# A decoder step on one core: both value products of a head pair issued one behind the other, behind the next unit's transposes

## The chip, the cores and the metric

The kernel is written in Bass for one core of a Trainium2 chip. It is one launch that fills five instruction queues by hand: TensorE (PE), ScalarE (ACT), VectorE (DVE), GpSimd (POOL) and SyncE (SP). Each queue runs in order, and semaphores tie them together. The metric is the device time of one launch in microseconds. The kernel before took 1098.66 us in the median of 3 runs (1098.1 to 1100.58). The execution that was profiled took 1095.08 us.

## The reference, cut to what matters

One hybrid decoder layer is computed for a prompt of 1024 tokens and for 8 samples of 8 tokens each, with the same weights. The part that matters here is the attention of the prompt. There are 8 blocks of 128 queries. For every block there are 8 NSA heads (two KV heads of four query heads each) with three branches, and 4 heads of attention into 256 memory tokens. Selection of blocks is no restriction here, since there are only 16 blocks and the 16 best are taken.

```
def gathered_attend(qb, kg, vg, mask):
    s = jnp.einsum('bqkgd,bkqsd->bkgqs', qb, kg) * SCALE
    p = masked_softmax(s, mask[:, :, None])
    return jnp.einsum('bkgqs,bkqsd->bqkgd', p.astype(vg.dtype), vg)

def window_attend(qb, t, kw, vw, kpos):
    s = jnp.einsum('bqkgd,bskd->bkgqs', qb, kw) * SCALE
    mask = (kpos[None, :] <= t[:, None]) & (kpos[None, :] > t[:, None] - WINDOW) & (kpos[None, :] >= 0)
    p = masked_softmax(s, mask)
    return jnp.einsum('bkgqs,bskd->bqkgd', p.astype(vw.dtype), vw)
```

In all branches the scores, the softmax and the product with the values are separate steps, and the results are `gates * o_c + gates * o_s + gates * o_w`. Around this part lie the input projection and the retention heads (the first 510 us), and the output projection with the last RMSNorm (the last 130 us).

## The kernel before, in words

**Units.** The prompt's attention is cut into NV = 144 units, 18 for each of the 8 query tiles (`UN = 18`). Tile i is the units 18i to 18i+17. A unit v holds the softmaxes of one head. Units come in pairs: the even unit v and the odd unit v+1 are the same branch for head g of the first KV head and head g of the second. Units 0, 1 of every four are the selected branch (i+1 key tiles of 128), units 2, 3 are the window branch (up to 5 key tiles) together with the compressed branch (one tile of 64 keys). The last two units of a tile (16, 17) hold the memory heads, two each.

**What is done for a unit.** On PE `qk(v)` computes scores into one of two PSUM areas (lines 1473, 1474, and 1476 for the mask). On DVE `maxima(v)` takes the row maximum (line 1798). On ACT the exponential writes the probabilities P[v % 2] into SBUF (line 1722). PE transposes the tiles of P in chunks of up to four tiles (line 1500) into PSUM bank 4 + c % 3, where c counts all chunks. ACT or DVE, in turns, copies a chunk out to one of six buffers PT (line 1661). PE then multiplies the values with the PT chunks of both units of a pair (line 1623), one chunk of the even unit with the same chunk of the odd unit: that is `pv(pair)`. When a group of six results is complete, ACT copies it out (`ot`, line 1748), PE transposes it back (chunk kind "o", line 1505), and DVE normalises it (`norm`, lines 1809 to 1814).

A pair of units has one chunk each, or two. The selected branch has two chunks from tile 4 on, the window branch from tile 3 on. In the text, C0 and C1 are the first and second chunk of an even unit, and A0, A1 and B0, B1 those of the even and the odd unit of the pair before it. pv(A0, B0) and pv(A1, B1) are the two products of that pair.

**What sets the order.** `schedule()` (line 1191 and on) writes one list of steps, and every engine walks through it and issues its part. For a unit v the steps are: `qk(v + 2)`; the chunks of v, each with `add_p`; the `pv` that are due; `sm(v + 2)`, which is maxima and exponential of the unit v + 2; then one group of steps of other work: transposes of the next tile's queries (chunk kind "q", line 1510, whose two-part copy is ACT line 1735 and DVE line 1891), or the samples' attention (kinds "mk", "kt", "st", "si", "sv" and so on, lines 1530 to 1598). These other chunks use the same three banks.

**The waits that matter.** A transposed chunk c waits until the chunk c - 3 was copied out of its bank. `qk(v + 2)` waits until the exponentials of unit v are done. `pv` waits until its chunks were copied. A copy into PT waits for the product that read that buffer six chunks ago. ACT and DVE run their steps in the list's order too.

**Where the change is.** Lines 1244 to 1256, in the loop over a unit's chunks. `waiting` is the list of pairs whose product is not issued yet, and `ranks` numbers the chunks of kind "p". Before, at most one product was issued behind each chunk, and only when the pair's last chunk lay two or more such chunks back.

Of the kernel before, what the change touches and what calls it, by code (L numbers as in the profile page):

```python
# [144 lines left out]
def build(nc, io):  # L145
# [1008 lines left out]
    def softmaxes(v):  # L1154

        i, l = v // UN, v % UN
        base = 1024 * (v % 2)
        if l >= 16:
            m = l - 16
            return [(24 + 2 * m + j, 24 + 2 * m + j, 3, 2 * m + j, 0, NM, [(base + 512 * j, NM)], 256 * j) for j in range(2)]  # L1160
        g, j = l // 4, l % 2
        h, k0 = g + 4 * j, 0 if l % 4 < 2 else max(0, i - WIN // 128)
        n = 128 * (i + 1 - k0)
        halves = [(base, n)] if n <= 512 else [(base, n // 2), (base + 512, n // 2)]
        if l % 4 < 2:
            return [(6 * g + j, 6 * g + j, 0, h, 0, n, halves, 0)]
        return [(6 * g + 2 + 2 * j, 6 * g + 2 + j, 1, h, k0, n, halves, 0), (6 * g + 3 + 2 * j, 6 * g + 4 + j, 2, h, 0, 64, [(base + 512 + 448, 64)], 640)]

    def tiles_of(v):

        return [(a, k, min(128, s[5])) for a, s in enumerate(softmaxes(v)) for k in range((s[5] + 127) // 128)]

    def sample_groups():

        groups = [[("t", ("sq",))]]
        for g in range(2):
            groups += [[("t", ("mk", b))] for b in range(4 * g, 4 * g + 4)]
            groups += [[("t", ("mq", g))], [("me", g)], [("t", ("mt", g))], [], [("t", ("mv", g)), ("load_mem", 1) if g == 0 else ("load_pair", 0)], [("store_mem", g)]]
        for p in range(NPAIR):
            groups += [[("t", ("sc", p))], [("ec", p)], [("nc", p)], [], [("t", ("si", p))]]  # L1180
            groups += [[("t", ("kt", p, c))] for c in (4, 5)]
            groups += [[("t", ("sw", p))], [("mw", p), ("t", ("kt", p, 0))], [("ew", p), ("t", ("kt", p, 2))], [("t", ("ss", p, 0))],
                       [("t", ("kt", p, 1))], [("t", ("kt", p, 3))], [("t", ("st", p, 2))], [("t", ("ss", p, 1))], [("ms", p)], [("es", p)],
                       [("t", ("st", p, 3))], [("t", ("st", p, 0))], [("t", ("st", p, 1))], [("t", ("sv", p))] + ([("load_pair", p + 1)] if p + 1 < NPAIR else []),
                       [("store_pair", p)]]
        groups += [[("load_fin", 0)], [], [("fin", 0)], [], [], [("load_w", 0)], [("load_w", 1)], [], []]
        for m in range(4):
            groups += [[("w_hi", m)], [("w_lo", m)] + ([("load_w", m + 2)] if m < 2 else []), []]
        return groups

    def schedule():

        chunks, steps, waiting, outs = [], [], [], []
        act_of, turn, ranks = [], [0], {}

        def add(c):  # L1200
            kind = c[0]
            copied = kind in ("p", "mk", "mt", "kt", "st")
            act_of.append(turn[0] % 2 == 0 if copied else kind == "sw")
            turn[0] += copied
            chunks.append(c)
            steps.append(("t", len(chunks) - 1))

        def add_p(v, tiles):
            add(("p", v, tiles))
            c = len(chunks) - 1  # L1210
            ranks[c] = len(ranks)
            for o in outs:
                o[1] += 1
            while outs and outs[0][1] >= 2:
                write(outs.pop(0)[0])
            return c

        def write(n):
            add(("o", n))
            steps.append(("norm", n))  # L1220

        def pv():
            pair = waiting.pop(0)
            steps.append(("pv", pair))
            v = chunks[pair[1]][1]
            a, k, _ = chunks[pair[1]][2][-1]
            if v % UN in (3, 7, 11, 15, 17) and a == 1 and 128 * (k + 1) >= softmaxes(v)[a][5]:
                n = NG * (v // UN) + (v % UN) // 4
                steps.append(("ot", n))
                outs.append([n, 0])  # L1230

        groups = sample_groups()
        first = 4
        for part in range(3):
            add(("q", 0, part))
        steps.append(("load_q", 2))
        for v in range(2):
            steps.extend([("qk", v), ("sm", v)])
        for v in range(NV):
            i, l = v // UN, v % UN  # L1240
            if v + 2 < NV:
                steps.append(("qk", v + 2))
            tiles = tiles_of(v)
            mine = []
            for f in range(0, len(tiles), 4):
                mine.append(add_p(v, tiles[f:f + 4]))
                if waiting and ranks[waiting[0][1]] + 2 <= ranks[mine[-1]]:
                    pv()
                if l >= 16:
                    waiting.append((mine[-1], mine[-1]))  # L1250
                elif l % 2:
                    waiting.append((partner[len(mine) - 1], mine[-1]))
            partner = mine
            if v + 2 < NV:
                steps.append(("sm", v + 2))
            if i >= 1 and i + 1 < QT and l == 5:
                steps.append(("load_z", i + 1))
            if i + 1 < QT and l in (9, 11, 13):
                add(("q", i + 1, (l - 9) // 2))
                if l == 13 and i + 3 < QT:  # L1260
                    steps.append(("load_q", i + 3))
            for what, n in groups.pop(0) if v >= first and groups else []:
                if what == "t":
                    add(n)
                else:
                    steps.append((what, n))
            if v == 2 * UN:
                steps.append(("copy_win", 0))
            if v % 4 == 0 and 2 * UN < v <= 2 * UN + 24:
                steps.append(("copy_kv", (v - 2 * UN) // 4 - 1))  # L1270
            if v == NV - 8:
                steps.extend([("load_m", 0), ("load_m", 1)])
            if v >= NV - 2:
                d = v - (NV - 2)
                steps.append(("load_x", d))
                for part in range(2):
                    add(("x", d, part))
        assert not groups
        for d in range(NT):
            steps.append(("d", d))  # L1280
            if d + 2 < NT:
                steps.append(("load_m", d + 2))
            if d == 0:
                while waiting:
                    pv()
                while outs:
                    write(outs.pop(0)[0])
            if d + 2 < NT:
                for part in range(2):
                    add(("x", d + 2, part))  # L1290
            steps.append(("y", d))
            if d + 2 < NT:
                steps.append(("load_x", d + 2))
        return chunks, steps, act_of

    p_chunks, p_steps, p_act = schedule()

    def chunk_act(c):
# [757 lines left out]
```

## Time and profile before

| | |
|---|---|
| median of 3 runs | 1098.66 us (1098.1 to 1100.58) |
| profiled execution | 1095.08 us, its span 1093.3 us |
| PE busy | 988.1 us, 90% of the span |
| DVE busy | 512.1 us, 47% |
| ACT busy | 390.4 us, 36% |
| POOL busy | 209.5 us, 19% |
| granted TensorE clock, mean | 0.973 of full |
| chain that ended last | PE 69%, DVE 8%, issue 7%, DMA 5%, ACT 5% |

"Busy" of PE counts the modelled time of matmuls, which overlap, so 90% busy is not 90% of what the array can do. PEld is the loading of weights, which is a row of its own: most matmuls here have one load each, and in a stream the loads stand end to end. "Issue" is time in which an engine waited for nothing that the profile shows. The time outside the span (1.8 us) is the same kind of overhead in any run. Times below are microseconds from the span's start. The prompt's attention runs from 514 to about 965.

### The profile page before, as it was taken

How to read it: one execution, taken by the hardware profiler on the slowest of the kernel's cores; microseconds unless marked ns; L12 is line 12 of the kernel's file. 1: busy time of each engine (PE TensorE's matmuls, PEld its weight loads, DVE VectorE, ACT ScalarE, POOL GpSimd, SP SyncE). 2: the span in 40 equal slices, each digit the busy share in tenths (PEclk: the TensorE clock that was granted, in tenths of full speed). 3: DMA queues.
4: the chain of work that ended last, by engine and by line, in shares of the span. 5: the costliest groups of instructions: out<-in, count | busy, mean ns of one | idle time of the engine just before them, and what ended most of it. 6: DMA issues, size and time to landing. Idle time of an engine off the chain costs nothing.

```text
span 1093.3 us, 20913 instructions
## 1 busy us (share of the span) xinstructions
PE 988.1 (90%) x8117; PEld 853.2 (78%) x8117; DVE 512.1 (47%) x1241; ACT 390.4 (36%) x961; POOL 209.5 (19%) x318
## 2 busy tenths in 40 slices
PE   1999999999999999998767888989898998999994
PEld 1999999999999999898555566666665776768883
DVE  4763332322225433362346557666655657634432
ACT  4432221142110121133335455555555557632210
POOL 1122221311152455412002012020010232002000
PEclk9999999999999999999689899999999999999997
DMA  7453431432425333173634484240330133013430
GB/s 197 158 196 101 143 114 62 143 76 95 128 71 138 110 116 102 35 175 103 158 108 123 139 271 114 56 156 1 91 98 1 52 97 128 18 49 125 147 123 38
DMA packets 100675, 119.15 MB, mean 109 GB/s; under 512 B 38770, under 2 KB 82706, under 8 KB 100002
## 3 DMA queue, kind: packets, MB, share of 16 engines
q1 hardware_dynamic: 88962, 78.44, 25.3%
q0 software_dynamic: 8704, 32.43, 8.5%
q10 hardware_dynamic: 2912, 6.95, 1.8%
q8 instruction: 65, 1.06, 0.4%
q14 instruction: 32, 0.26, 0.1%
HBM read 92.72 MB, written 32.02 MB: 114 GB/s over the span
## 4 chain that ended last, share of the span: by engine, by line
PE 69%; DVE 8%; issue 7%; DMA 5%; ACT 5%; SPq 3%; POOL 2%; ACTq 0%; DVEq 0%; POOLq 0%
PE psum L501 10%; PE psum L502 9%; PE psum L503 9%; PE psum L1500 4%; PE psum L1623 4%; PE psum L1473 3%; DVE p_nb L1798 3%; PE psum L1639 3%; PE psum L1640 3%; PE psum L1641 3%; ACT p_P L1722 2%; PE psum L1474 2%; PE psum L723 2%; PE psum L725 2%; PE psum L724 2%
## 5 line engine op out<-in xcount | busy, mean ns | idle before, releaser
L501 PE MATMUL psum<-a_whi,f_xhi 128*128 128x256 f32 (+2 forms) x968 | 279.8, 289 | 0.0
L502 PE MATMUL psum<-a_wlo,f_xhi 128*128 128x256 f32 (+2 forms) x968 | 274.2, 283 | 0.0
L503 PE MATMUL psum<-a_whi,f_xlo 128*128 128x256 f32 (+2 forms) x968 | 273.3, 282 | 0.0
L501 PEld LDWEIGHTS psum<-a_whi,f_xhi 128*128 128x128 f32 (+1 forms) x968 | 178.2, 184 | 2.7 <-issue 0.9
L502 PEld LDWEIGHTS psum<-a_wlo,f_xhi 128*128 128x128 f32 (+1 forms) x968 | 178.2, 184 | 0.0
L503 PEld LDWEIGHTS psum<-a_whi,f_xlo 128*128 128x128 f32 (+1 forms) x968 | 178.1, 184 | 0.0
L1722 ACT ACTIVATE p_P<-psum,p_nb 128x640 f32<-128x640 f32 (+7 forms) x224 | 123.8, 557 | 138.9 <-DVE p_nb L1798 128.5
L638 POOL DMA_DIRECT2D h_scratch<-a_hst x117 | 64.5, 553 | 262.5 <-DVE a_hst L940 176.8
L1500 PE MATMUL psum<-f_ident,p_P 128*128 128x128 f32 (+1 forms) x656 | 108.3, 285 | 5.9 <-DVE p_QB L1891 4.8
L1798 DVE TENSOR_REDUCE p_nb<-psum 128x1 f32<-128x640 f32 (+7 forms) x224 | 109.7, 520 | 4.3 <-PE psum L1476 3.3
L1661 DVE COPY p_PT<-psum 128x512 f32<-128x512 f32 (+4 forms) x108 | 56.3, 521 | 92.5 <-PE psum L1500 92.1
L1473 PE MATMUL psum<-p_KS,p_QA 128*128 128x320 f32 (+5 forms) x192 | 78.4, 409 | 12.1 <-ACT p_P L1722 9.8
L1623 PE MATMUL psum<-p_PT,p_V 128*64 128x128 f32 x1056 | 79.8, 284 | 0.9 <-ACT p_PT L1661 0.9
L1500 PEld LDWEIGHTS psum<-f_ident,p_P 128*128 128x128 f32 (+1 forms) x656 | 70.3, 142 | 12.8 <-DVE p_QB L1891 6.3
L1951 POOL TENSOR_TENSOR p_zt<-f_OC,p_zt 128x256 f32<-128x256 f32 x8 | 5.8, 724 | 384.5 <-DVE p_Oi L1814 384.5
L949 DVE TENSOR_TENSOR c_ctlo<-psum,c_cthi 128x512 fp32r<-128x512 f32 (+1 forms) x40 | 25.4, 636 | 106.1 <-ACT c_cthi L853 106.1
L1661 ACT COPY p_PT<-psum 128x512 f32<-128x512 f32 (+4 forms) x108 | 55.5, 514 | 41.4 <-PE psum L1500 41.2
L1623 PEld LDWEIGHTS psum<-p_PT,p_V 128*64 128x64 f32 x1056 | 56.1, 137 | 18.0 <-issue 15.8
L853 ACT CAST c_cthi<-psum 128x512 fp32r<-128x512 f32 (+1 forms) x40 | 21.8, 544 | 124.7 <-PE psum L706 124.7
L1474 PE MATMUL psum<-p_KS,p_QB 128*128 128x320 f32 (+5 forms) x192 | 64.3, 336 | 0.0
L1473 PEld LDWEIGHTS psum<-p_KS,p_QA 128*128 128x128 f32 x192 | 38.1, 199 | 30.9 <-ACT p_P L1722 16.5
L1639 PE MATMUL psum<-d_whi,d_xh 128*128 128x512 f32 (+1 forms) x144 | 57.6, 400 | 0.0
(290 smaller groups left out, 1757.8 us busy)
## 6 DMA issues: line engine op xcount, KB each, us to landing
a_wraw<-in_w_in SPq DMA_DIRECT2D x24, 512.0 KB, 5.4
h_scratch<-a_hst POOLq DMA_DIRECT2D x96, 128.0 KB, 2.1
s_SG<-in_cache_nsa_slc SPq DMA_DIRECT2D x64, 128.0 KB, 2.2
a_xraw<-in_x_prompt SPq DMA_DIRECT2D x8, 512.0 KB, 3.5
p_qd<-h_scratch SPq DMA_DIRECT2D x16, 256.0 KB, 3.9
s_MK<-in_cache_mem SPq DMA_DIRECT2D x8, 512.0 KB, 5.7
mix_scratch<-p_zt POOLq DMA_DIRECT2D x8, 512.0 KB, 3.0
s_WG<-in_cache_nsa_win SPq DMA_DIRECT2D x8, 512.0 KB, 5.8
```

Source lines behind the costliest of these rows:

```text
L501: nc.tensor.matmul(out, hi, wh, start=first, stop=False)
L502: nc.tensor.matmul(out, hi, wl, start=False, stop=False)
L503: return nc.tensor.matmul(out, lo, wh, start=False, stop=last)
L638: pool.dma_start(dst, hst[n % HST][0:r, 0:w]).then_inc(S(f"h_out{n % HST}"), 16)
L1473: nc.tensor.matmul(o, QA[i % 2][:, hq, :], k, start=True, stop=False)
L1474: l = nc.tensor.matmul(o, QB[i % 2][:, hq, :], k, start=False, stop=not masks)
L1500: l = nc.tensor.transpose(o[0:w, 128 * j:128 * j + 128], P[v % 2][:, at:at + w], ident[:])
L1623: i_mm = nc.tensor.matmul(psum[64 * j:64 * j + 64, at:at + 128], val, PTs[p_rank[pair[j]] % NPT][0:w, 128 * p:128 * p + 128], start=k == 0 ...
L1639: nc.tensor.matmul(o, hi, dwhi[jj][:, k], start=k == 0, stop=False)
L1661: copy(PTs[r % NPT][0:w, 0:128 * n], bank(4 + c % 3)[0:w, 0:128 * n]).then_inc(sem, 1)
L1722: nc.scalar.activation(dst, s_view(s), ACT.Exp, bias=nb[:, g % NNB:g % NNB + 1], accum_out=ssum[:, i % 2, s[1]:s[1] + 1]).then_inc(S("p_ex ...
L1798: nc.vector.tensor_reduce(out=nb[:, g % NNB:g % NNB + 1], in_=s_view(s), op=ALU.max, axis=AX.X if len(s[6]) == 1 else AX.XY, negate=True). ...
```

## The change

The product is no longer issued inside the loop over chunks. Behind all chunks of a unit, products are issued as long as there are any that don't need a chunk of this same unit, and only if the unit is even within its tile, or one of the two memory units.

```diff
             for f in range(0, len(tiles), 4):
                 mine.append(add_p(v, tiles[f:f + 4]))
-                if waiting and ranks[waiting[0][1]] + 2 <= ranks[mine[-1]]:
-                    pv()
                 if l >= 16:
                     waiting.append((mine[-1], mine[-1]))
                 elif l % 2:
                     waiting.append((partner[len(mine) - 1], mine[-1]))
             partner = mine
+            while waiting and (l % 2 == 0 or l >= 16) and waiting[0][1] not in mine:
+                pv()
             if v + 2 < NV:
                 steps.append(("sm", v + 2))
```

The first place is a window unit with two chunks in tile 6, on PE. p_P_118 are the probabilities of the even unit, p_PT_132 and p_PT_128 the copied chunks A0 and B0, p_PT_143 and p_PT_129 the chunks A1 and B1. Before:

```order
L1500 MATMUL psum<-f_ident,p_P_118 128x128 x4
L1623 MATMUL psum<-p_PT_132,p_V 64x128
L1623 MATMUL psum<-p_PT_128,p_V 64x128
...
L1500 MATMUL psum<-f_ident,p_P_118 128x128
L1500 MATMUL psum<-f_ident,p_P_118 64x128
L1623 MATMUL psum<-p_PT_143,p_V 64x128
L1623 MATMUL psum<-p_PT_129,p_V 64x128
...
L1582 MATMUL psum<-f_ident,s_PSl 128x128 x4
```

The same place now:

```order
L1500 MATMUL psum<-f_ident,p_P_118 128x128 x5
L1500 MATMUL psum<-f_ident,p_P_118 64x128
L1623 MATMUL psum<-p_PT_132,p_V 64x128
L1623 MATMUL psum<-p_PT_128,p_V 64x128
...
L1623 MATMUL psum<-p_PT_143,p_V 64x128
L1623 MATMUL psum<-p_PT_129,p_V 64x128
...
L1582 MATMUL psum<-f_ident,s_PSl 128x128 x4
```

The first product moved from between C0 and C1 to behind C1, and stands directly ahead of the second product. There are 32 such places, all in tiles 4 to 7.

The second place is a pair with one chunk per unit, in tile 1, on PE. p_P_118 and p_P_119 are the probabilities of the even and the odd unit, p_PT_128 and p_PT_129 the copied chunks of the pair before. Before:

```order
L1500 MATMUL psum<-f_ident,p_P_118 128x128 x2
L1473 MATMUL psum<-p_KS,p_QA_115 128x256
L1474 MATMUL psum<-p_KS,p_QB_117 128x256
L1476 MATMUL psum<-p_maskb,f_identb 128x128
L1473 MATMUL psum<-f_KCp,p_QA_115 128x64
L1474 MATMUL psum<-f_KCp,p_QB_117 128x64
L1476 MATMUL psum<-p_maskb,f_identb 128x64
L1500 MATMUL psum<-f_ident,p_P_119 128x128 x2
L1623 MATMUL psum<-p_PT_128,p_V 64x128
L1623 MATMUL psum<-p_PT_129,p_V 64x128
```

The same place now:

```order
L1500 MATMUL psum<-f_ident,p_P_118 128x128 x2
L1623 MATMUL psum<-p_PT_128,p_V 64x128
L1623 MATMUL psum<-p_PT_129,p_V 64x128
...
L1473 MATMUL psum<-p_KS,p_QA_115 128x256
L1474 MATMUL psum<-p_KS,p_QB_117 128x256
L1476 MATMUL psum<-p_maskb,f_identb 128x128
...
L1500 MATMUL psum<-f_ident,p_P_119 128x128 x2
```

The product moved from the odd unit up into the even unit, ahead of the next scores. With it the copy of finished results on ACT (line 1748) and the "o" transposes (line 1505) come one unit earlier in these tiles.

The third place is the end of tile 5 on PE, with the two memory units. p_PT_130 and p_PT_131 are memory chunks, and p_VM is the memory's values. Before, the product with p_PT_143 and p_PT_129 stands in the second memory unit, and both memory products in the first unit of the next tile:

```order
L1623 MATMUL psum<-p_PT_128,p_V 64x128
L1473 MATMUL psum<-p_KS,p_QA_114 128x448
...
L1500 MATMUL psum<-f_ident,p_P_119 128x128 x4
L1623 MATMUL psum<-p_PT_143,p_V 64x128
L1623 MATMUL psum<-p_PT_129,p_V 64x128
...
L1500 MATMUL psum<-f_ident,p_P_118 128x128 x4
L1623 MATMUL psum<-p_PT_130,p_VM 64x128 x4
L1500 MATMUL psum<-f_ident,p_P_118 128x128 x3
L1505 MATMUL psum<-f_ident,p_OT 128x128 x3
L1623 MATMUL psum<-p_PT_131,p_VM 64x128 x4
```

The same place now:

```order
L1623 MATMUL psum<-p_PT_143,p_V 64x128
L1623 MATMUL psum<-p_PT_129,p_V 64x128
...
L1473 MATMUL psum<-p_KS,p_QA_114 128x448
...
L1500 MATMUL psum<-f_ident,p_P_119 128x128 x4
L1623 MATMUL psum<-p_PT_130,p_VM 64x128 x4
...
L1500 MATMUL psum<-f_ident,p_P_118 128x128 x4
L1505 MATMUL psum<-f_ident,p_OT 128x128 x3
L1500 MATMUL psum<-f_ident,p_P_118 128x128 x3
L1623 MATMUL psum<-p_PT_131,p_VM 64x128 x4
```

Every product moved up by one place, and the "o" transposes stand between the two chunks of the next tile's first unit. The queues of SP and POOL are unchanged.

## Rows read from the trace of the kernel before

**Rows 1.** Busy time by stretch: PE, PEld, DVE, ACT, POOL, granted clock, DMA share, GB/s.

```profile
514.00:640.00 126.00, 96.03 (x775) 71.18 (x775) 65.68 (x207) 58.21 (x206) 13.85 (x24) 0.84 0.51 146
718.00:965.00 247.00, 222.96 (x2075) 167.43 (x2076) 154.53 (x338) 137.32 (x340) 31.80 (x31) 1.00 0.21 64
965.00:1093.00 128.00, 112.85 (x553) 88.58 (x549) 44.33 (x100) 25.04 (x53) 10.70 (x15) 0.96 0.29 103
```

**Rows 2.** Waits, 514 to 640: engine, waited for, total us, times, longest.

```profile
PE psum L1530 <- DMA s_MK<-in_cache_mem: 10.7, 2, 7.9
```

**Rows 3.** Waits of the weight loads, 718 to 965, same columns.

```profile
PEld psum L1623 <- issue: 13.9, 80, 0.2
PEld psum L1473 <- ACT p_P L1722: 9.8, 16, 1.4
PEld psum L1500 <- DVE p_QB L1891: 5.8, 6, 1.9
PEld psum L1500 <- issue: 4.8, 27, 0.3
```

**Rows 4.** Time line around one window unit of tile 6: start, us, engine.

```profile
873.42 0.42 PEld L1500 LDWEIGHTS psum<-f_ident,p_P 128*128 128x128 f32 x4
874.01 0.85 PEld L1623 LDWEIGHTS psum<-p_PT,p_V 128*64 128x64 f32 x16 [0.17 <-issue]
874.01 1.09 PE L1623 MATMUL psum<-p_PT,p_V 128*64 128x128 f32 x16
874.03 0.94 DVE L1798 TENSOR_REDUCE p_nb<-psum 128x1 f32<-128x640 f32 x2
875.04 0.17 PEld L1500 LDWEIGHTS psum<-f_ident,p_P 128*128 128x128 f32 x2 [0.17 <-issue]
875.04 0.44 PE L1500 MATMUL psum<-f_ident,p_P 128*128 128x128 f32 x2
875.51 0.42 DVE L1661 COPY p_PT<-psum 128x256 f32<-128x256 f32 x1 [0.53 <-PE psum L1500]
875.85 1.08 DVE L1798 TENSOR_REDUCE p_nb<-psum 128x1 f32<-128x896 f32 x1
878.18 0.19 PEld L1473 LDWEIGHTS psum<-p_KS,p_QA 128*128 128x128 f32 x1 [0.33 <-ACT p_P L1722]
```

**Rows 5.** Time line of the weight loads, 869 to 872.

```profile
869.97 0.19 PEld L1623 LDWEIGHTS psum<-p_PT,f_VC 64*64 64x64 f32 x4 [0.17 <-issue]
871.43 0.76 PEld L1500 LDWEIGHTS psum<-f_ident,p_P 128*128 128x128 f32 x7
```

**Rows 6.** Time line, the three units whose second chunk came late.

```profile
756.63 0.17 PEld L1500 LDWEIGHTS psum<-f_ident,p_P 128*128 128x128 f32 x2 [1.66 <-DVE p_QB L1891]
...
819.35 0.42 PEld L1500 LDWEIGHTS psum<-f_ident,p_P 128*128 128x128 f32 x4
821.54 0.69 DVE L1891 SCALAR_TENSOR_TENSOR p_QB<-psum,p_QA 128x512 fp32r<-128x512 f32 x1 [1.80 <-ACT p_QA L1735]
822.28 0.17 PEld L1500 LDWEIGHTS psum<-f_ident,p_P 128*128 128x128 f32 x2 [1.49 <-DVE p_QB L1891]
...
839.58 0.17 PEld L1500 LDWEIGHTS psum<-f_ident,p_P 128*128 128x128 f32 x2 [1.91 <-DVE p_QB L1891]
```

**Rows 7.** Time line, weight loads of scores that waited, first and last of seven.

```profile
797.04 0.19 PEld L1473 LDWEIGHTS psum<-p_KS,p_QA 128*128 128x128 f32 x1 [0.68 <-ACT p_P L1722]
...
940.14 0.19 PEld L1473 LDWEIGHTS psum<-p_KS,p_QA 128*128 128x128 f32 x1 [0.94 <-ACT p_P L1722]
```

**Rows 8.** Time line, one of seven units whose bank came free at the last moment.

```profile
886.04 0.42 PEld L1500 LDWEIGHTS psum<-f_ident,p_P 128*128 128x128 f32 x4
886.15 0.56 DVE L1814 TENSOR_TENSOR p_Oi<-psum,p_rw 128x384 f32<-128x384 f32 x1
```

**Rows 9.** Time line in tile 0: copy of an odd unit's chunk, next transposes.

```profile
518.80 0.29 DVE L1661 COPY p_PT<-psum 128x128 f32<-128x128 f32 x1 [1.02 <-PE psum L1500]
519.29 0.64 PE L1500 MATMUL psum<-f_ident,p_P 128*128 128x128 f32 x2
```

## The prediction

> **What bounds the kernel now.** I read the busy time by stretch first. The clock is granted in full from 718 to 965, PE is busy 223.0 of 247 us there, DVE 154.5 and ACT 137.3 [rows 1]. So PE is nearly the bound in tiles 4 to 7, but not alone: the waits of that stretch show the loads of scores standing 9.8 us for the exponentials, and the loads of transposes 5.8 us for a bank that DVE empties [rows 3]. From 514 to 640 PE is busy only 96.0 of 126 us at a mean clock of 0.84, and single waits for memory loads are as long as 7.9 us [rows 1, 2]. What is gained ahead of such a wait is lost at it. From 965 on the rest is mostly PE work [rows 1], and a shift of its start passes to the end.
>
> Then the time line of one window unit with two chunks. Four loads of transposes end at 873.84, and the first load of the product stands at 874.01, behind 0.17 of idle. The product's 16 loads take 0.85, and the next transposes start at 875.04, behind 0.17 again [rows 4]. The matmuls start with their loads (874.01 and 875.04), so the gap delays the array as well, and is not hidden under a matmul. That gap comes where the array's shape changes, 128*128 to 128*64 or back. It also comes inside one product, from 128*64 to 64*64, where there is no semaphore to wait for; and seven transposes that belong to two chunks, with waits between them, load in 0.76 without a gap [rows 5]. So it is the shape and not the wait that costs.
>
> **The change part by part.**
>
> *Changes of shape.* In the 32 units with two chunks of tiles 4 to 7, C0, product, C1, product becomes C0, C1, product, product. That is one entry into the narrow shape and one exit fewer. Over the whole order there are 114 runs of products before and 79 now; counting every boundary between full, half and quarter shape, there are 62 fewer. The profile has 27 exits towards transposes with 4.8 us of idle, 0.18 each [rows 3], and 0.17 in the unit shown [rows 4]. I take 62 times 0.17 = 10.5 us of PE time.
>
> The Trainium skill has two rules on this that point apart. "TensorEngine Tiling (Array Packing)", section Key Properties, says that changing the tiling mode drains TensorE. "TensorE: Matmul & The Clock Gate", in its opening table, says that the queue pulls weight loads ahead of matmuls in flight. By the first the sum stays as it is, by the second the loads behind a change would be ready and the gain would be nothing; the rows agree with the first.
>
> *C1 loses its cover.* C1 must wait until the chunk three back has left its bank. Before, the first product lay in between and hid 0.85 + 2 x 0.17 = 1.19 us of this. In 28 of the 32 units C1 did not wait at all, beyond the gap. In three it did: the waits of 1.66, 1.49 and 1.91 at 756.63, 822.28 and 839.58 [rows 6]. There the bank holds a chunk of queries, which needs a copy on ACT and then one on DVE: at 821.54 DVE starts, 1.8 us after C0's loads ended at 819.77 [rows 6]. This copy does not depend on where the product stands. So C1 starts when it did, and the product's 0.85 comes on top: 3 x 0.85 = 2.6 us lost. Their six gaps lay inside the waits and give nothing, 1.0 us less. The remaining unit of the 32 waited for a copy that its product waited for too, and does not change.
>
> *Who waits behind.* A PE wait at C1 holds both products, then the sample transposes and the next scores, and on ACT the copy of finished results (line 1748) with the exponentials behind it. This is in the 0.85.
>
> *C1 comes earlier.* In the other units C1 starts 1.02 earlier. Its copy stands ahead of the next even unit's maximum on DVE: the chain copy at 875.51, maximum 875.85, then exponential and, at 878.18, the scores that waited 0.33 for it, hangs on it [rows 4]. Here DVE had another maximum until 874.97 [rows 4], so half of the 1.02 would arrive. In tiles 5 to 7 scores issued in an even unit, whose exponentials hang on such a chain, waited seven times for over half a microsecond, 7.6 us in all [rows 7]. Bounds: nothing comes back, or all 7.6. I take a third, 2.5, since in most of these the chain hangs on other work of ACT or DVE too.
>
> *Gains that a later wait takes.* 56 gaps x 0.17 = 9.5 us are gone, but PE runs into its waits for ACT and DVE [rows 3] sooner, and there the gain stays only if the releaser came earlier as well. Bounds: nothing is taken, or all 9.5. I take 3.4, somewhat over a third, since PE waits in about every second pair.
>
> *Tiles 0 to 3.* The product moves from the odd into the even unit. Its chunks must be copied by then. The tightest place is in tile 0: the copy ends at 519.09, and the two transposes behind which the product now stands start at 519.29 and are issued by 519.6, so 0.5 us is left [rows 9]. The "o" transposes, copy and normalisation move with it, in the same sequence. I cost this at nothing; the cover is the time of the scores between. If it is gone, 24 such pairs that miss by 0.1 cost 2.4 us, part of which a memory wait swallows [rows 2].
>
> *Sum.* -9.5 + 2.6 + 3.4 - 2.5 = -6.0 us against the profiled 1095.08, so 1089.1. The median of the runs shown lies 3.6 higher than that execution, and I give the forecast on the median: 1098.66 - 6.0 = 1092.7. "Same" below means within 0.2%, 2.2 us, which is about what a measurement of this kernel can tell.
>
> **The rivals.**
>
> *Everything pays.* All 9.5 of gaps stays, and the earlier C1 removes most of the waits of its chain: -9.5 + 2.6 - 5 = about -12, or 1086.7. For it speaks that PE is the busiest by far [rows 1]; against it that DVE and ACT hold PE up in the same tiles [rows 3].
>
> *The gain is swallowed.* PE, DVE and ACT are close to a common rhythm, and all 9.5 are taken back at the next waits: 2.6 - 2.5 = about zero, 1098.8. For it speaks that the waits on ACT and DVE come every few units [rows 3].
>
> *The banks become the bound, and it is slower.* The three late units are not the only ones near the edge. In seven the bank came free less than 0.4 before C0's loads ended, or just behind: in the one shown the normalisation ends at 886.71, and C0's loads at 886.46 [rows 8]. If PE gets ahead of DVE, all ten expose the product: 10 x 0.85 = 8.5 lost, and 20 gaps worth 3.4 fall inside waits, so 7.1 is left of the 10.5. With 3.4 swallowed as above that is +8.5 - 7.1 + 3.4 = +4.8, or 1103.5. It decides when the bank comes free later than C0's end; up to there C1 costs nothing, and from a whole product's length later the full 0.85 is lost. Against it speaks that in most of the seven PE itself starts the copy, two or three blocks earlier, so that it would move along.
>
> *The change does not do what it says.* If the gap came from the wait ahead of each product, both gaps would stay between the two products and in front of C1, and only the 2.6 would be left: 1101.3. Rows 5 speak against it.
>
> **How the numbers follow.** Forecast 0.46, everything pays 0.23, swallowed 0.16, banks 0.11, not what it says 0.04. The forecast's own range is 1089 to 1097, from a sum with the two thirds halved or doubled. The range for 8 in 10 takes in most of "everything pays" and half of "swallowed": 1085 to 1100. Faster by over 0.2% is nearly all of the first two and a little of the third: 0.70. Same is the middle of "swallowed" and the upper edge of the forecast: 0.17. Slower is the last two: 0.13.
>
> **What would show it.** Right: the idle of L1500 put down to issue between 718 and the end of this stretch falls from 4.8 to near nothing, that of L1623 falls by some 27 entries from 80, transposes load in groups of five to eight, and the time line shows 24 or more narrow loads in a row. Three waits of about 2.5 us stand ahead of C1 where queries were transposed before. The stretch of tiles 4 to 7 is some 5 us shorter, the one after 965 unchanged in length. Wrong: more than five waits over 1 us ahead of C1, or a product that waits for its copy in tiles 0 to 3, or loads that keep their 0.17 between two products; any of these turns the sign or takes the gain.

## The result and the profile after

| | before | after |
|---|---|---|
| median | 1098.37 us (16 runs) | 1091.30 us (16 runs) |
| lowest, highest | 1094.77, 1104.25 | 1088.13, 1096.65 |
| profiled execution | 1095.08 | 1088.52 |
| its span | 1093.3 | 1086.7 |

The ratio of after to before is 0.9933, with a 95% interval of 0.9915 to 0.9951. That is 7.4 us less, 5.4 to 9.3. The two spans differ by 6.6.

The busy time of the changed kernel by stretch answers to [rows 1]; the columns are the same.

```profile
514.00:640.00 126.00, 95.38 (x768) 70.15 (x768) 65.01 (x205) 57.68 (x203) 14.24 (x25) 0.84 0.48 138
718.00:965.00 247.00, 220.07 (x2135) 173.30 (x2134) 157.37 (x343) 140.92 (x353) 31.75 (x31) 1.00 0.23 70
965.00:1086.00 121.00, 106.67 (x494) 84.06 (x492) 41.41 (x94) 21.44 (x43) 10.69 (x15) 0.96 0.27 98
```

In the same 247 us PE, DVE and ACT get through more: PE 2135 matmuls instead of 2075. Its busy time is nevertheless 2.9 us lower. Matmul ends are modelled, and part of a gap is drawn as work of the matmul ahead of it (in [rows 4] the product's matmuls end at 875.10, behind the next load's start at 875.04). Line 1623 is busy 73.2 us over the whole run for its 1056 matmuls with p_V, and was busy 79.8 for the same 1056. So the busy time misleads here, and the count of matmuls is the better reading. The first matmul of the output projection (line 1639) starts at 963.0 instead of 969.0. The projection itself keeps its length: its last weight load starts at 1071.2 instead of 1077.7.

The waits of the weight loads in that stretch answer to [rows 3].

```profile
PEld psum L1623 <- issue: 9.6, 54, 0.2
PEld psum L1500 <- DVE p_QB L1891: 9.4, 7, 2.7
PEld psum L1473 <- ACT p_P L1722: 8.0, 12, 1.4
...
PEld psum L1473 <- DVE p_PT L1661: 2.4, 2, 1.6
```

The gaps ahead of products fell from 80 to 54. The 27 gaps ahead of transposes (4.8 us) are no longer in the list. In their place the transposes wait 9.4 us for the banks instead of 5.8. The scores wait 8.0 for the exponentials instead of 9.8.

The time line of the unit of [rows 4], number 114 of all units, shows it piece by piece.

```profile
869.28 0.19 PEld L1473 LDWEIGHTS psum<-p_KS,p_QA 128*128 128x128 f32 x1
...
870.22 0.61 PEld L1500 LDWEIGHTS psum<-f_ident,p_P 128*128 128x128 f32 x6
...
871.03 1.51 PEld L1623 LDWEIGHTS psum<-p_PT,p_V 128*64 128x64 f32 x28 [0.20 <-issue]
...
871.69 0.41 DVE L1661 COPY p_PT<-psum 128x256 f32<-128x256 f32 x1
...
872.02 1.08 DVE L1798 TENSOR_REDUCE p_nb<-psum 128x1 f32<-128x896 f32 x1
...
873.10 0.19 PEld L1473 LDWEIGHTS psum<-p_KS,p_QA 128*128 128x128 f32 x1 [0.56 <-ACT p_P L1722]
...
874.64 0.19 PEld L1473 LDWEIGHTS psum<-p_KS,p_QA 128*128 128x128 f32 x1
```

The unit's first scores in the kernel before:

```profile
872.48 0.19 PEld L1473 LDWEIGHTS psum<-p_KS,p_QA 128*128 128x128 f32 x1
```

Six transposes load in one piece, then 28 narrow loads behind a single gap of 0.20. Before there were three gaps in the same work. C1's copy starts 2.41 us behind the start of the unit's first scores; before it was 3.03 (875.51 less 872.48). The even unit's scores for the next pair then start at 874.64, 5.36 behind, instead of 5.70.

The three units of [rows 6] wait longer for their bank now.

```profile
756.26 0.17 PEld L1500 LDWEIGHTS psum<-f_ident,p_P 128*128 128x128 f32 x2 [2.55 <-DVE p_QB L1891]
...
820.45 0.17 PEld L1500 LDWEIGHTS psum<-f_ident,p_P 128*128 128x128 f32 x2 [2.50 <-DVE p_QB L1891]
...
825.20 0.20 PEld L1486 LDWEIGHTS psum<-s_KTs,s_QP 128*64 128x64 f32 x4 [0.64 <-ACT p_PT L1661]
826.21 0.19 PEld L1473 LDWEIGHTS psum<-p_KS,p_QA 128*128 128x128 f32 x1 [0.81 <-issue]
...
837.47 0.17 PEld L1500 LDWEIGHTS psum<-f_ident,p_P 128*128 128x128 f32 x2 [2.75 <-DVE p_QB L1891]
```

**Where the 6.6 us are.** The order is fixed, so both time lines can be cut at the same instruction. I cut at the first scores that each even unit issues (the start of the matmul of line 1473), and take the time from one cut to the next (one even and one odd unit). No scores follow the last pair of the table, that of unit 140, so it is cut at the first transposes of unit 142. These lengths repeat to 0.02 us in nearly every pair between the profiled executions of two kernels that order the pair alike, so differences of 0.3 can be read. Differences to the kernel before, in us, over tiles 4 to 7 and the memory units ahead of them, with the sum at the end; all are worked out from the time lines:

```
                        after  e1     e7     e2     e5     e4     e6     e3     e8
13 units that gain     -5.08  -3.48  +0.02  +0.01  -5.58  +5.80  -1.82  -5.07  -5.07
9 units, no change     -0.20  +0.37  -0.12  -0.13  +3.23  +1.87  +0.40  -0.53  -0.67
units 102, 118, 122    +0.32  +0.12  +0.84  +0.43  +2.53  -1.17  +1.95  -0.04  +0.49
late: 82, 100, 104     +0.38  +1.57   0.00  -0.02  +0.85  -2.30  +4.06  -0.39  -0.36
first unit of a tile   -2.91  -2.93  -2.90  -2.91  -2.90  -2.89  -2.90  -2.91  -2.74
memory units           +0.89  -0.01  +0.88  +0.89  +0.89  +0.89  +1.45  +0.89  +1.08
sum                    -6.59  -4.36  -1.26  -1.74  -0.98  +2.20  +3.14  -8.05  -7.26
```

In e1, e5 and e6 the clock fell for some 3 us at two places each (the last section), which is 2.8, about 4 and 3.1 us of their sums. In e8 it fell once, which is about 0.3. Unit 118 is the least steady: it is at +0.2 in the changed kernel and at -0.1 in a second execution of it (a2).

Two things brought time in the changed kernel. In 28 even units (seven per tile, the first of the tile left out) the two chunks stand together with both products behind them, and that is worth 4.6 net. In the first unit of a tile, which brings the places of the section on the change to 32, only one product (a memory product) is left, and the "o" transposes stand between C0 and C1. At the four places where a tile ends and the next begins, the new order is worth 2.0 net.

### The profile page after: what moved, and what is told of

It is laid out like the page before. It is cut to its first block, busy times and chain, and to the rows that moved or that the text cites. A ratio compares the mean times of both kernels' runs of the same rounds, so it can differ in the third digit from the quotient of the medians.

```text
span 1086.7 us, 20914 instructions
## 1 busy us (share of the span) xinstructions
PE 975.5 (90%) x8117; PEld 852.4 (78%) x8117; DVE 510.6 (47%) x1241; ACT 390.6 (36%) x961; POOL 208.3 (19%) x318
## 4 chain that ended last, share of the span: by engine, by line
PE 72%; DVE 8%; issue 6%; DMA 5%; ACT 4%; SPq 3%; POOL 1%; ACTq 0%; DVEq 0%; POOLq 0%
PE psum L501 10%; PE psum L502 10%; PE psum L503 10%; PE psum L1623 5%; PE psum L1500 5%; PE psum L1473 3%; PE psum L1640 3%; PE psum L1641 3%; PE psum L1639 3%; PE psum L1474 3%; DVE p_nb L1798 2%; ACT p_P L1722 2%; PE psum L723 2%; PE psum L725 2%; PE psum L724 2%
## 5 line engine op out<-in xcount | busy, mean ns | idle before, releaser
L1500 PE MATMUL psum<-f_ident,p_P 128*128 128x128 f32 (+1 forms) x656 | 103.8, 282 | 11.6 <-DVE p_QB L1891 9.6
L1623 PE MATMUL psum<-p_PT,p_V 128*64 128x128 f32 x1056 | 73.2, 282 | 0.5 <-ACT p_PT L1661 0.5
L1623 PEld LDWEIGHTS psum<-p_PT,p_V 128*64 128x64 f32 x1056 | 57.0, 138 | 12.5 <-issue 10.9
```

The lines of the kernel that those rows point to most:

```text
L1500: l = nc.tensor.transpose(o[0:w, 128 * j:128 * j + 128], P[v % 2][:, at:at + w], ident[:])
L1623: i_mm = nc.tensor.matmul(psum[64 * j:64 * j + 64, at:at + 128], val, PTs[p_rank[pair[j]] % NPT][0:w, 128 * p:128 * p + 128], start=k == 0 ...
```

## The experiments

The columns of the table are named by the first two letters of the runs; e9 is not in it. The lines of the experiments' kernels stand 0 to 6 further down than in the kernel after (1502, 1503 or 1506 for 1500, and so on). All ratios are against the kernel before, on the same chip.

**a2: the change once more.** Nothing is edited.

> The changed kernel once more, as the base for the three runs beside it. Every theory: 6 to 9 us faster than before.

Measured: 0.9932 (0.9912 to 0.9952), 7.5 us less. The pair lengths are those of after within 0.02, but for three pairs, and sum to -6.8.

**e1 and e2: the change in two parts.** In e1 only the even units with two chunks, the tile's first among them, take the new order. In e2 all the rest does, and these units, but for the tile's first, keep the product between C0 and C1. Against after:

```
e1:
+            both = l % 2 == 0 and l < 16 and len(tiles) > 4 and len(waiting) == 2
             for f in range(0, len(tiles), 4):
                 mine.append(add_p(v, tiles[f:f + 4]))
+                if not both and waiting and ranks[waiting[0][1]] + 2 <= ranks[mine[-1]]:
+                    pv()
...
-            while waiting and (l % 2 == 0 or l >= 16) and waiting[0][1] not in mine:
+            while both and waiting and waiting[0][1] not in mine:
e2:
+            split = l % 2 == 0 and l < 16 and len(tiles) > 4 and len(waiting) == 2
...
+                if split and f == 0:
+                    pv()
```

> Only the 32 even units with two chunks are changed (C0, C1, product, product); tiles 0 to 2, the memory units and the window pairs of tile 3 keep the old rule. Theory (changes of array shape): nearly the whole gain is here, 64 gaps of 0.17 less in the trace, -6 to -8 us against the kernel before, all of it in tiles 4 to 7, with the three waits of about 2.5 us ahead of C1 as after the change. Rival (the moved products of tiles 0 to 2 and of the memory units bring it): within 2 us of before.

> The complement: the 32 units keep product between C0 and C1, everything else is moved as in the change. Theory: within 2 us of before, the window of tiles 4 to 7 as long as before, at most 1.5 us gained from six fewer runs of products. Rival (placement in the one-chunk tiles matters): 4 us or more faster.

Measured: e1 0.9966 (0.9945 to 0.9987), 3.7 us less; e2 0.9963 (0.9945 to 0.9981), 4.1 us less. Together that is 7.8, against 7.4 for the whole. But the parts overlap: both have the 2.9 of the tile's first units (why is told under e7). And e1 lost 2.8 to the clock in the profiled execution. What the table adds is where e2 gains: at the tile's ends alone, and 0.01 in the 13 units.

**e7: only the tile's ends.** The new rule holds in the memory units and in the tile's first unit alone.

```
+            ends = l >= 16 or l == 0
...
+                if not ends and waiting and ranks[waiting[0][1]] + 2 <= ranks[mine[-1]]:
+                    pv()
...
-            while waiting and (l % 2 == 0 or l >= 16) and waiting[0][1] not in mine:
+            while ends and waiting and waiting[0][1] not in mine:
```

> Only the two memory units of each tile and the first unit of the next follow the new rule; all else is as before the change. It is a part of the part that the complement run moved. Theory A (the ends of tiles bring what that run gained, by products that leave a crowded first unit and by one run less): 2 to 4 us faster than before, gained in tiles 4 to 7. Theory B (tiles 0 to 3 bring it, by products and result transposes one unit earlier): within 1.5 us of before.

Measured: 0.9969 (0.9952 to 0.9986), 3.4 us less. This is the same as e2 within the interval, so the ends carry e2's gain, and tiles 0 to 3 bring none that can be told. How it comes about is seen at the start of tile 6. Weight loads of the kernel before, with two lines of DVE:

```profile
849.01 0.19 PEld L1473 LDWEIGHTS psum<-p_KS,p_QA 128*128 128x128 f32 x1 [0.58 <-ACT p_P L1722]
...
851.29 0.31 PEld L1500 LDWEIGHTS psum<-f_ident,p_P 128*128 128x128 f32 x3 [0.17 <-issue]
851.57 0.36 PEld L1505 LDWEIGHTS psum<-f_ident,p_OT 128*128 128x128 f32 x3
852.28 0.17 DVE L1809 TENSOR_SCALAR p_rw<-p_ssum 128x6 f32<-128x6 f32 x1 [0.77 <-PE psum L1505]
...
853.38 0.95 DVE L1798 TENSOR_REDUCE p_nb<-psum 128x1 f32<-128x640 f32 x2
...
856.13 0.42 PEld L1582 LDWEIGHTS psum<-f_ident,s_PSl 128*128 128x128 f32 x4 [1.09 <-ACT p_PT L1661]
```

The same place in e7:

```profile
849.27 0.42 PEld L1626 LDWEIGHTS psum<-p_PT,p_VM 128*64 128x64 f32 x8 [0.17 <-issue]
849.86 0.19 PEld L1476 LDWEIGHTS psum<-p_KS,p_QA 128*128 128x128 f32 x1 [0.17 <-issue]
...
852.21 0.42 PEld L1626 LDWEIGHTS psum<-p_PT,p_VM 128*64 128x64 f32 x8 [0.17 <-issue]
...
856.11 0.42 PEld L1585 LDWEIGHTS psum<-f_ident,s_PSl 128*128 128x128 f32 x4 [0.50 <-ACT p_PT L1664]
```

Before, PE stood 0.58 for exponentials ahead of the first unit's scores. A memory product, 0.42 and a gap of 0.17, now stands in just that hole, and the pair of the memory units keeps its length (5.22, then 5.24). Ahead of tiles 4 and 5 there is no such hole, and the memory pair pays 0.58 and 0.29. The tile's first pair falls from 7.53 to 6.67. Line 1582 waits 0.50 for ACT's copy instead of 1.09.

What shortens this pair is not the second chunk coming earlier. In e4 (below) C1 stands behind the memory product that is left. Its lines at this place, where the scores start at 850.59:

```profile
852.09 0.36 PEld L1507 LDWEIGHTS psum<-f_ident,p_OT 128*128 128x128 f32 x3
...
853.21 0.31 PEld L1502 LDWEIGHTS psum<-f_ident,p_P 128*128 128x128 f32 x3 [0.17 <-issue]
...
854.10 0.95 DVE L1800 TENSOR_REDUCE p_nb<-psum 128x1 f32<-128x640 f32 x2
```

C1 starts 2.62 behind the first scores, and 2.28 before the change: it is later. The pair takes 6.67 all the same. What came earlier is the "o" transposes, 1.50 behind the scores instead of 2.56. Before, DVE idled 0.77 for them, and on DVE the normalisation of the results stands ahead of the next maximum. That maximum starts 3.51 behind the scores instead of 4.37, which is 0.86 earlier, and the pair is 0.86 shorter. In tiles 4, 5 and 7 the maximum comes 0.65, 0.62 and 0.76 earlier, in e4 as in the change, and the pairs are 0.65, 0.62 and 0.77 shorter. e1 keeps both memory products in this unit, but puts them behind the "o" transposes: there the maximum comes 0.72 to 0.74 earlier, and the four pairs gain 2.93. So the 2.9 comes of the memory product no longer standing ahead of the "o" transposes.

**e4: both products between C0 and C1.** The changes of shape are as few as in the change, but C1 comes later, by the length of the second product as well.

```
                 mine.append(add_p(v, tiles[f:f + 4]))
+                while f == 0 and l % 2 == 0 and l < 16 and len(tiles) > 4 and waiting:
+                    pv()
```

> The change, but in the 32 units both products stand between C0 and C1. The number of shape changes is that of the changed kernel (two per unit), but C1 now comes later than before (by the second product, 0.3 to 0.6 us) instead of 1.0 us earlier, and the three late banks are covered by two products. Theory (the gaps are the gain, the earlier C1 little): as fast as the changed kernel or up to 2.6 us faster, -7 to -10 us against before. Rival (the earlier C1, with the copy, maximum and exponential behind it, is what pays): within 2 us of before or slower, with more waits of scores for exponentials.

Measured: 1.001 (0.9991 to 1.0029), 1.1 us more than before and 8.5 more than the change. Its waits of the weight loads from 718 to 965:

```profile
PEld psum L1475 <- ACT p_P L1724: 15.2, 14, 1.5
```

The scores wait 15.2 us for exponentials, against 8.0 in after. In unit 114, shown above for the change, two engines' time line of e4 reads:

```profile
873.44 0.19 PEld L1475 LDWEIGHTS psum<-p_KS,p_QA 128*128 128x128 f32 x1 [0.87 <-ACT p_P L1724]
...
874.96 1.51 PEld L1625 LDWEIGHTS psum<-p_PT,p_V 128*64 128x64 f32 x28 [0.17 <-issue]
876.64 0.17 PEld L1502 LDWEIGHTS psum<-f_ident,p_P 128*128 128x128 f32 x2 [0.17 <-issue]
...
877.12 0.42 DVE L1663 COPY p_PT<-psum 128x256 f32<-128x256 f32 x1 [2.01 <-PE psum L1502]
877.46 1.08 DVE L1800 TENSOR_REDUCE p_nb<-psum 128x1 f32<-128x896 f32 x1
...
879.79 0.19 PEld L1475 LDWEIGHTS psum<-p_KS,p_QA 128*128 128x128 f32 x1 [1.43 <-ACT p_P L1724]
```

DVE idles 2.01 for C1, and its copy stands 3.68 behind the start of the scores (873.44), where after has 2.41, and the pair takes 6.35. In after it takes 5.36. This is the chain of [rows 4]: C1, its copy, the maximum queued behind that copy, the exponential, the scores. Over the 13 units e4 is 10.9 slower than the change, and over the nine 2.1. It is ahead in the late units (2.7), where both products hide the wait, and in units 102, 118 and 122 (1.5).

**e5: C1 early, but each product alone.** The second product is held back to the odd unit: C0, C1, product; D0, D1, product. There are nearly as many gaps as before: in tiles 4 to 7 the weight loads of e5 stand 150 times behind an idle time of 0.15 to 0.21, against 166 times before and 111 in the change (e4: 115). C1 is as early as in the change.

```
+            hold = l % 2 == 0 and l < 16 and len(tiles) > 4 and len(waiting) == 2
...
-            while waiting and (l % 2 == 0 or l >= 16) and waiting[0][1] not in mine:
+            while waiting and (l % 2 == 0 or l >= 16 or late) and waiting[0][1] not in mine:
                 pv()
+                late = False
+                if hold:
+                    late = True
+                    break
```

> The change, but in the 32 pairs the second product moves behind the odd unit's chunks: C0, C1, product, then D0, D1, product. C1 is early as in the change, but each product stands alone, so the shape changes are as many as before (32 more runs of products than in the change). Theory (gaps): all of the 9.5 us of gaps is back, the three late banks cost 2.6, and the earlier C1 gives 2 or 3: within 2 us of before. Rival (the earlier C1 pays): still 5 us or more faster than before.

Measured: 0.9948 (0.9930 to 0.9967), 5.7 us less; the change has 7.4. From e2, which has the gaps and the late C1, it is 1.4 ahead in the medians, and the change is another 1.7 ahead of it. The intervals overlap in both cases, so the medians don't say how the gain is shared. They do say that with the products placed so the gaps cost far less than the 9.5 that they last.

**e6: the gaps put back.** A small matmul in the full shape stands between the two products of 32 places. It adds to columns of a bank that nobody reads; the rest is the change.

```
+            if v >= 4 * UN and l < 16 and v % 2 == 0 and len(tiles_of(v)) > 4 and p_chunks[pair[0]][2][0][:2] == (0, 0):
+                nc.tensor.matmul(psum[:, 512 * 7 + 384:512 * 7 + 448], identb[:], maskb[:, 0:64], start=False, stop=False, skip_group_check=True)
             i_mm.then_inc(S("p_pv"), 1)
```

> The change, with one small full-shape matmul (128 rows by 128 columns of weights, 64 columns moved, into columns of PSUM that nobody reads) between the two products of the 32 units. Nothing moves, only the array changes shape twice more per unit: 32 x (0.34 and 0.03 to 0.10 for the matmul itself) = 12 to 14 us of PE time. Theory as the earlier runs now have it (about 4 of 10 us of gaps reach the end, the rest is taken back at waits for ACT and DVE): 4 to 7 us slower than the changed kernel. Rival 1 (PE alone bounds, every gap counts): 11 us or more slower. Rival 2 (gaps cost nothing, the earlier C1 is all): within 2 us of it.

Measured: 1.0005 (0.9989 to 1.0022), 8.3 us slower than the change run beside it. Weight loads of unit 114 in e6:

```profile
879.30 0.85 PEld L1623 LDWEIGHTS psum<-p_PT,p_V 128*64 128x64 f32 x16 [0.20 <-issue]
880.32 0.10 PEld L1626 LDWEIGHTS psum<-p_maskb,f_identb 128*128 128x128 bf16 x1 [0.17 <-issue]
880.46 0.64 PEld L1623 LDWEIGHTS psum<-p_PT,p_V 128*64 128x64 f32 x12
```

A gap of 0.17 stands ahead of the small matmul, with no semaphore near it. From the end of the first product's loads (880.15) to the second's start it is 0.31. 31 of them lie in the pairs of the table. That is 9.6 us of PE time put in, and 9.7 come out in the sum. But this is not all the gaps' doing. In two of the late units the clock fell behind the wait. The stretches of e6 there, with the granted clock as the third number from the end:

```profile
755.00:758.00 3.00, 0.68 (x7) 0.44 (x6) 1.20 (x4) 2.15 (x6) 0.00 (x0) 1.00 0.00 0
758.00:762.00 4.00, 4.00 (x31) 3.20 (x31) 1.63 (x3) 1.47 (x3) 0.00 (x0) 0.68 0.01 4
```

and its weight loads:

```profile
758.00 0.17 PEld L1500 LDWEIGHTS psum<-f_ident,p_P 128*128 128x128 f32 x2 [2.56 <-DVE p_QB L1893]
...
760.15 0.72 PEld L1582 LDWEIGHTS psum<-f_ident,s_PW 128*128 128x128 f32 x4 [0.33 <-issue]
760.85 0.34 PEld L1473 LDWEIGHTS psum<-p_KS,p_QA 128*128 128x128 f32 x1
```

Four transposes load in 0.72 instead of 0.42, and the gap is 0.33. The pairs of units 82 and 104 lengthen by 1.82 and 1.86, of which 0.31 each is the insertion. Without the 3.1 that are left, 6.6 of 9.6 arrive: about two thirds of PE time put in here is paid. In unit 114 nothing is (5.37 against 5.36), and in eleven of the 13 units that gain 0.27 to 0.29 is.

This divides the gain of the 13 units. With the change's order and the gap put back, 1.8 of their 5.1 stays, 0.7 of it in unit 92, and 3.3 is the gap's. As a whole, though, e6 is no faster than the kernel before and 4.6 slower than e2, in which the gaps are there and C1 is late (by the pairs, without the 3.1 of the clock, 0.0 against -1.7). So with the gaps in place the new order of the 28 units brought no gain in sum.

**e3: the cover kept.** In the three late units one product goes back between C0 and C1.

```
                 mine.append(add_p(v, tiles[f:f + 4]))
+                if v in (82, 100, 104) and f == 0:
+                    pv()
```

> The change, but in the three units whose second bank comes free late (the units 82, 100 and 104) the first product stays between C0 and C1. Theory (a late bank exposes the product's 0.85): 2.6 us faster than the changed kernel, -9 to -11 us against before, with waits ahead of C1 of about 1.5 us instead of 2.5. Rival (what PE gains at these places is lost at the next wait for ACT or DVE): within 1 us of the changed kernel.

Measured: 0.9914 (0.9888 to 0.9940), 9.4 us less than before. The medians put it 1.8 ahead of the change run beside it, with overlapping intervals; the sum of the pairs 1.5. Of these, 1.4 are in the pairs of units 82, 84, 102 and 104, and none in that of 100. The time lines tell why. Loads of e3 in unit 100:

```profile
817.93 0.42 PEld L1502 LDWEIGHTS psum<-f_ident,p_P 128*128 128x128 f32 x4
818.52 0.85 PEld L1625 LDWEIGHTS psum<-p_PT,p_V 128*64 128x64 f32 x16 [0.17 <-issue]
820.86 0.17 PEld L1502 LDWEIGHTS psum<-f_ident,p_P 128*128 128x128 f32 x2 [1.49 <-DVE p_QB L1893]
...
825.61 0.20 PEld L1488 LDWEIGHTS psum<-s_KTs,s_QP 128*64 128x64 f32 x4 [1.29 <-ACT p_PT L1663]
```

Here C1 waits 1.49 and the sample scores of line 1488 then wait 1.29. In after these were 2.50 and 0.64, with the transposes of line 1510 no longer waiting 0.26 in between. From C0's start to the next even scores it is 8.69 either way (826.62 less 817.93, and 826.21 less 817.52). ACT's copy sets this unit, and what the cover loses is taken out of a later wait.

**e8 and e9: more cover.** e8 puts both products ahead of C1 in these three units, e9 in units 84 and 118 as well.

```
+                while v in (82, 100, 104) and f == 0 and waiting:
+                    pv()
```

> The change, but in the three units with a late second bank (82, 100, 104) both products stand between C0 and C1. Theory (what counts there is how much of the late bank's wait has work over it, and the gaps stay at two): about 1.7 us of the second product's time is hidden as well, 2 to 3 us faster than the kernel that keeps one product there, -11 to -12 us against before; the waits ahead of C1 fall to about 1 us or less. Rival (C1 later is bad everywhere, as in the run with all 32 units): as slow as the changed kernel or slower.

> The same with two more units (84 and 118), whose second bank came free 0.2 us before, and 0.2 us behind, C0's end in the trace of before. Theory (it pays only where the bank is late by more than a gap): no faster than the kernel with three units, within 1 us of it, since 1.0 us of C1's lead is given up for nothing. Rival (any unit whose bank is near its limit pays): 1 us or more faster than it.

Measured: e8 0.9929 (0.9909 to 0.9949), 7.8 us less; e9 0.9928 (0.9902 to 0.9955), 7.9 less. Loads of e8 in unit 82:

```profile
753.86 1.07 PEld L1625 LDWEIGHTS psum<-p_PT,p_V 128*64 128x64 f32 x20 [0.17 <-issue]
756.26 0.17 PEld L1502 LDWEIGHTS psum<-f_ident,p_P 128*128 128x128 f32 x2 [1.32 <-DVE p_QB L1893]
756.85 0.42 PEld L1584 LDWEIGHTS psum<-f_ident,s_PW 128*128 128x128 f32 x4 [0.43 <-DVE s_KTs L1675]
...
759.39 0.42 PEld L1512 LDWEIGHTS psum<-f_ident,p_qd 128*128 128x128 f32 x4 [0.83 <-ACT s_PTS L1681]
```

C1 waits 1.32 (1.53 in e3), but PE then stands 0.43 and 0.83 for copies. The pair takes 8.41, and in e3 8.40. So the idea that more cover buys more falls: the first product buys what there is. That e8 is 1.6 worse than e3 by the ratios is within the intervals, and the pairs show only 0.8 of it, 0.5 of that in the unsteady unit 118 and 0.3 behind its one fall of the clock. The pairs of e9 sum to -7.8.

## Why the prediction held, step by step

It gave 1092.7 and 6.0 us less; measured were 1091.3 and 7.4 (5.4 to 9.3). The mechanism was right for the 28 units, not for the tile's ends, and the sum is nearer than its parts. Its terms against the profiled pairs, over tiles 4 to 7:

| step | predicted | in the trace |
|---|---|---|
| 25 units not late: two gaps each | -8.5 | -8.5 removed |
| taken by later waits, less what the earlier C1 returns | +3.4 - 2.5 = +0.9 | +3.5 |
| three late units | +2.6 | +0.4 |
| first unit of a tile and memory units (6 of the 62 gaps) | -1.0 | -2.0 |
| tiles 0 to 3 | 0 | none that can be told |
| sum | -6.0 | -6.6 |

**Changes of shape.** The gap is the shape's, as [rows 5] said: the six transposes behind each other have none, 28 narrow loads have one, and e6 gets it back without a wait. In tiles 4 to 7, 55 idle times of this length are gone (166 to 111), and the prediction counted 56 + 6. The price of one here is 0.17 at the full clock. What a gap is worth is another matter. Nine of the 25 units gain nothing; in five of them one wait for ACT or DVE grew by 0.2 to 0.3 instead (in unit 86 from 1.87 to 2.17). Of the two rules of the Trainium skill that the prediction weighed, the runs stay with that of "TensorEngine Tiling (Array Packing)", Key Properties, that a change of the tiling mode drains TensorE.

**C1 earlier, and gains taken.** Both were sized by guess (a third of 7.6, a third of 9.5), and this is where the sum was weakest. The net was +3.5 instead of +0.9. The two are not even separate terms. With the same gain at the tile's ends in both, e4 removes the gaps and loses 1.1, and e5 keeps most of them and gains 5.7. In the 13 units both things count. Nine of these pairs gain 0.29 to 0.35, about the two gaps (0.34), and in eight of them e6 takes 0.28 to 0.29 back by PE work that stands behind C1. That the place of C1 counts too is seen in e4, where six of these pairs hold a wait for exponentials of 0.87 to 1.54, and in unit 92: it gains 0.96 (5.49 to 4.53), while e6 is still at 4.80, e5 at 4.84 and e4 at 5.93.

**The lost cover.** The three waits came as forecast, 2.55, 2.50 and 2.75 against "about 2.5". Together they are 2.7 longer than in [rows 6], which is the 2.6. The step failed in taking a longer wait for lost time. Unit 100 lost nothing, as shown; the three pairs lost 0.4 in all. Against e3 the change gives away 1.5 by the pair lengths, not 2.6; by the medians the two can't be told apart.

**Tiles 0 to 3.** No product waits for its copy there, so the 0.5 us of [rows 9] sufficed. One long wait for the memory's load stands near the end of tile 0 (7.0 us, and 7.9 before the change), and the lengths ahead of it differ by 1 to 2 us between the executions. A few tenths can't be read in that.

**The rivals.** "Swallowed" (0) and "banks" (+4.8) lie outside the interval. "Everything pays" (-12) does too, though e3 comes within 3 of it. "Not what it says" is refuted by the 28 loads in a row. None of them, nor the forecast, had the first unit of a tile, where the earlier "o" transposes brought 2.9. The forecast had put their move at nothing for tiles 0 to 3 and had no term for it in tiles 4 to 7. That the sum came out near is in part luck: it put the net cost of the gains taken and the earlier C1 2.6 too low, the cost of the late units 2.2 too high, and the gain at the tile's ends 1.0 too low.

**What stays open.** How the 4.6 of the 28 units divide between gaps and C1's place is settled by e6 for the 13 units alone (3.3 and 1.8). For the whole, e6 and e5 disagree: both have an early C1 and gaps, and e5 is 6.2 us ahead of e6 by the ratios. It moves one product into the odd unit, and gets its next scores out sooner by that. What this is worth by itself no run shows. Whether e3 really is 2 us ahead of the change would take more runs. It is the best median of the study, and the late units of the pair lengths agree with it.

## What to carry to other kernels

Group PE work by array shape, but place the group by the chains that other engines wait for: the same merge gained 7.4 us with C1 ahead of it and lost 1.1 with C1 behind it. Look for such chains beyond the work that is moved. At four places a memory product stood ahead of a few result transposes, for which DVE's next maximum had to wait in the end, and that alone was 2.9 us. Before pricing a longer wait, look for the next wait on the same engine; in unit 100 one followed for a copy of another engine, and the price was nothing. A product moved into a wait of 0.58 cost nothing either.

## What the runs showed of the hardware

**Beside some waits of 1.6 to 2.8 us the clock fell, and beside others as long it did not.** From 718 to 965 the kernels before and after were granted the full clock throughout. In other runs it fell to half, each time for some 3 us, at the end of a wait or soon behind it: in e6 with waits of 2.56 and 2.75, in e1 of 2.01 and 2.50, in e5 of 1.98 and 2.21, in a2 and e8 of 1.56. e5 behind the wait of 1.98:

```profile
768.00:770.00 2.00, 1.22 (x17) 1.06 (x19) 1.79 (x5) 1.44 (x3) 0.00 (x0) 1.00 1.24 245
770.00:774.00 4.00, 4.00 (x27) 3.08 (x22) 1.78 (x6) 1.61 (x5) 0.00 (x0) 0.57 0.16 27
774.00:778.00 4.00, 4.00 (x43) 3.33 (x42) 2.88 (x8) 2.22 (x7) 0.00 (x0) 1.00 0.01 4
```

Its price was 1.2 to 2.0 us per pair where PE was the bound (unit 86 of e5: 8.48, and 6.50 in after). It was next to nothing where PE would have waited: a2 had 0.60 from 902 to 906, and that pair took 6.85 against 6.84 (7.02 in e8). In after, waits of 2.55, 2.50 and 2.75 left the clock at full. Of the thirteen waits of 2.5 or more in after, a2, e1, e5 and e6, three had a fall with them. So a longer wait may carry a risk beside its price. How large it is, one profiled execution of each kernel does not show.

**The gap scales with the clock:** 0.17 at the full clock, 0.33 at half, for the same change of shape.
